# Attention of two layers: heads worked in pairs, with the values as stationary operand in two column tiles and the division by the row sums moved ahead of the transpose to GpSimd

## The reference, cut to what matters

```
for layer in range(2):
    h = rms_norm(x, g_mix[layer]);  qkv = h @ w_in[layer]
    o_a = differential_attention(...)   # 4 heads: a = softmax(q1 k1) - lam * softmax(q2 k2); o = a @ v, normed per head
    o_b = moba_attention(...)           # 4 heads, computed here as plain causal attention
    o_c = dilated_attention(...)        # 8 heads, computed here with an additive log-count mask ("strip")
    x = x + concatenate([o_a, o_b, o_c]) @ w_out[layer]
    x = x + conv_gated_mlp(...)
```

## Time and profile before

| what | value |
|---|---|
| median of 3 runs | 2205.19 us (2205.01 to 2206.89) |
| the profiled execution's own time | 2204.52 us |
| its span | 2202.7 us |
| PE busy | 2150.4 us, 98% |
| DVE / ACT / POOL busy | 1501.5 / 946.7 / 1197.0 us |
| attention of the first of the two layers | 1024.7 to 1130.0 us from the span's start |
| attention of the second | 1674.9 to 1780.1 us |
| granted PE clock | 0.996 of 2.4 GHz over the span |

### The profile page before, as it was taken

One profiled execution on the slowest core, in us unless ns is written; L12 is line 12 of the kernel. 1 busy time (PEld: TensorE's weight loads), 2 busy tenths in 40 slices (PEclk: granted clock), 3 DMA queues, 4 the chain that ended last, 5 costly groups with the idle time before them and its releaser, 6 DMA issues.

```text
span 2202.7 us, 33160 instructions
## 1 busy us (share of the span) xinstructions
PE 2150.4 (98%) x12377; PEld 1837.3 (83%) x12377; DVE 1501.5 (68%) x2234; ACT 946.7 (43%) x1891; POOL 1197.0 (54%) x594
## 2 busy tenths in 40 slices
PE   6999999999999999999999999999999999999997
PEld 4787888787899988897887898888897887888886
DVE  6844877654666692897737677677996728777676
ACT  3264663112465600645744555412555725555312
POOL 4766404765576677654026545577653037544675
PEclk9999999999999999999999999999999999999998
DMA  8322103422232343232002232322221012223221
GB/s 324 152 77 96 58 21 115 172 96 77 77 114 99 115 158 115 78 114 77 1 20 79 94 115 77 115 96 95 96 97 58 1 39 85 92 93 115 96 96 58
DMA packets 32776, 206.78 MB, mean 94 GB/s; under 512 B 4080, under 2 KB 4336, under 8 KB 11632
## 3 DMA queue, kind: packets, MB, share of 16 engines
q1 hardware_dynamic: 32192, 200.27, 24.8%
q10 hardware_dynamic: 432, 4.46, 0.5%
HBM read 202.61 MB, written 2.10 MB: 93 GB/s over the span
## 4 chain that ended last, share of the span: by engine, by line
PE 87%; DVE 6%; issue 1%; DMA 1%; ACT 1%; DVEq 1%; POOL 1%; POOLq 1%; SPq 0%; ACTq 0%
PE PS L1126 18%; PE PS L1128 18%; PE PS L1127 18%; PE PS L1605 5%; PE PS L1617 5%; PE PS L1381 3%; PE PS L1382 3%; PE PS L1383 3%; PE PS L1631 3%; PE PS L1457 2%; PE PS L1459 2%; PE PS L1458 2%; PE PS L1256 1%; PE PS L1259 1%; PE PS L1258 1%
## 5 line engine op out<-in xcount | busy, mean ns | idle before, releaser
L665 POOL TENSOR_TENSOR w_hi<-raw,zero_c 128x512 fp32r<-128x512 f32 (+1 forms) x135 | 281.6, 2104 | 536.0 <-PE PS L1128 534.5
L669 POOL TENSOR_TENSOR w_lo<-raw,w_hi 128x512 fp32r<-128x512 f32 (+1 forms) x135 | 366.2, 2731 | 5.8
L1126 PE MATMUL PS<-b_hi,w_hi 128*128 128x512 f32 x512 | 203.1, 397 | 0.9 <-POOL w_lo L888 0.9
L1127 PE MATMUL PS<-b_lo,w_hi 128*128 128x512 f32 x512 | 203.0, 396 | 0.0
L1128 PE MATMUL PS<-b_hi,w_lo 128*128 128x512 f32 x512 | 203.0, 396 | 0.0
L3346 DVE TENSOR_TENSOR b_lo<-a_all,b_hi 128x512 fp32r<-128x512 f32 x44 | 162.5, 3733 | 49.3 <-ACT b_hi L2491 49.3
L1126 PE MATMUL PS<-f_hi,w_hi 128*128 128x512 f32 x448 | 177.6, 397 | 0.7 <-DVE f_lo L2648 0.7
L1128 PE MATMUL PS<-f_hi,w_lo 128*128 128x512 f32 x448 | 177.6, 396 | 0.0
L1127 PE MATMUL PS<-f_lo,w_hi 128*128 128x512 f32 x448 | 177.6, 396 | 0.0
L688 POOL TENSOR_TENSOR w_lo<-raw,w_hi 128x512 fp32r<-128x512 f32 x48 | 71.0, 1478 | 90.5 <-ACT w_hi L2483 90.5
L1126 PEld LDWEIGHTS PS<-b_hi,w_hi 128*128 128x128 f32 x512 | 96.4, 188 | 24.6 <-POOL w_lo L888 1.1
(11 more groups left out here) (586 smaller groups left out, 6858.8 us busy)
## 6 DMA issues: line engine op xcount, KB each, us to landing
raw<-slabs_dram SPq DMA_DIRECT2D x161, 1024.0 KB, 4.8
aux<-ada_dram SPq DMA_DIRECT2D x18, 512.0 KB, 5.4
ada_first<-ada_dram SPq DMA_DIRECT2D x11, 512.0 KB, 14.0
cmpw<-cmpw_dram ACTq DMA_DIRECT2D x2, 2048.0 KB, 11.5
ada_late<-ada_dram SPq DMA_DIRECT2D x8, 512.0 KB, 3.2
ada_last<-ada_dram SPq DMA_DIRECT2D x8, 512.0 KB, 5.6
xT<-xT_dram SPq DMA_DIRECT2D x1, 2048.0 KB, 9.0
out_dram<-t SPq DMA_DIRECT2D x4, 512.0 KB, 3.2
```

Source lines behind the costliest of these rows:

```text
L665: high = nc.gpsimd.tensor_tensor(w_hi[:, slot, c], raw[:, slot, c], zero[:, 0:c.stop - c.start], ALU.add)
L669: low = nc.gpsimd.tensor_tensor(w_lo[:, slot, c], raw[:, slot, c], w_hi[:, slot, c].bitcast(f32), ALU.subtract)
L1126: nc.tensor.matmul(out, a_hi_, b_hi_, start=start, stop=False)
L1127: nc.tensor.matmul(out, a_hi_, b_lo_, start=False, stop=False)
```

## The change

Work is now laid out in units. A unit is a *pair* (the same block of queries of two plain or two dilated heads), a *diff* (the two score tiles of one differential head), a *turn* (two of the late turns of queries and keys) or *out* (the turns of the two 128-wide blocks of differential outputs). Each unit has two of four PSUM score banks; turns follow three units later, values four, the finish five. What happens to a pair:

- DVE takes the reciprocals of the two row sums as soon as both exponentials are there (`weigh`), and POOL multiplies both tiles of probabilities by them in place (`scale_pairs`), before the turn.
- PE turns both tiles; ACT copies the first and DVE the second.
- In the product with the values the values are now the stationary operand (64 columns) and the turned probabilities the moving one (128 columns). The first head's result goes to partitions 0 to 63, the second's to 64 to 127 of one bank: two column tiles. Features now lie on the partitions, so a group of two heads is a finished 128-wide block of `o_hi`/`o_lo` without another turn, and without `finish`.

Differential heads keep their product as it was, and the two blocks that they fill keep their turn. Their join is now made for each tile by itself. POOL splits the first two slabs of `w_out` during the attention, in pieces of 512 columns, one piece after the scaling of each pair but the first. The first slab's product with `w_out` (eight banks) begins, for four banks, between the last turns and values. Some pairs of semaphores are merged to make room; that is left out here.

```diff
+        LAG_T, LAG_V, LAG_OUT = 3, 4, 5
+        W_MASKED, W_PROBS, W_TURNED = 4, 8, 4
...
+        def two_units():
+            units, groups = [], [Group(n, b) for n, b in enumerate((4, None, 5, None, 0, 1, 2, 3))]
+            singles = {1: (8, 9), 2: (10, 11), 4: (12, 13), 5: (14, 15)}
+            for i in (0, 1):
+                for n, j in enumerate((3, 0, 2, 1)):
+                    units.append(Unit("pair", plain_jobs[2 * i:2 * i + 2], j, groups[2 * i]))
+                    for half in (0, 1):
+                        units.append(Unit("diff", diff_jobs[2 * i + half:2 * i + half + 1], j, groups[2 * i + 1], half))
+                    if 4 * i + n in singles:
+                        units.append(Unit("turn", items=singles[4 * i + n]))
+            for i in range(4):
+                for j in (3, 0, 2, 1):
+                    units.append(Unit("pair", dilated_jobs[2 * i:2 * i + 2], j, groups[4 + i]))
+            units.insert(DIFF_AT + 7, Unit("out", items=(6, 7)))
...
+            def pieces_of(n):                                        # POOL
+                pool.wait_ge(slab_loaded[slot], 16 * nth + 16)
+                pool.wait_ge(slab_used, n - 1)
+                for a in range(0, SLAB, PIECE):
...
+            def scale_pairs(n, plan, layer):                         # POOL
+                pieces = itertools.chain(pieces_of(n), pieces_of(n + 1))
+                for u in plan.units:
+                    if u.kind != "pair":
+                        continue
+                    pool.wait_ge(inverted, plan.pairs * layer + u.pair + 1)
+                    inv = pair_inv(u)
+                    for c in (0, 1):
+                        p = w_probs(u.score + c, 128 * u.nb)
+                        last = nc.gpsimd.tensor_scalar(p, p, inv[:, c:c + 1], None, ALU.mult)
+                    last.then_inc(scaled_probs, 1)
+                    if u.pair > 0:
+                        next(pieces, None)
...
+                def values(u):                                       # PE
+                    pe.wait_ge(copied_act, at_.acopies + u.on_act)
+                    if u.kind == "pair":
+                        pe.wait_ge(copied_dve, at_.dcopies + u.on_dve)
...
+                    for b in range(u.nb):
+                        if u.kind == "pair":
+                            for c in (0, 1):
+                                last = nc.tensor.matmul(PS[64 * c:64 * c + 64, bank, 128 * u.j:128 * u.j + 128],
+                                                        u.jobs[c]["v"](u.lo + b),
+                                                        w_turned(u.tile + c, 512)[:, 128 * b:128 * b + 128],
+                                                        start=b == 0, stop=b == u.nb - 1)
...
+                for t in range(len(plan.units) + LAG_V):             # PE
+                    u = plan.at(t)
+                    if u is not None:
+                        front(u)
+                    else:
+                        tail(t - len(plan.units))
+                    for lag, part in ((LAG_T, turns), (LAG_V, values)):
...
+                def weigh(u):                                        # DVE
+                    dve.wait_ge(probs_ready, g0 + u.score + 2)
+                    a = sum_at(u, 0)
+                    if u.kind == "pair":
+                        V.reciprocal(pair_inv(u), SUMS[:, a:a + 2]).then_inc(inverted, 1)
+                        return
...
+                    then(V.reciprocal(r, SUMS[:, b:b + 1]))
+                    then(V.scalar_tensor_tensor(out=r, in0=r, scalar=lam_c, in1=SUMS[:, a:a + 1], op0=ALU.mult,
+                                                op1=ALU.mult))
+                    V.scalar_tensor_tensor(out=two, in0=two, scalar=r, in1=one, op0=ALU.mult, op1=ALU.add
+                                           ).then_inc(combined, 1)
```

More of the change, by code:

```diff
@@ L19 @@
+import itertools
 import math
@@ L556, in build, with __init__ @@
         block = ctx.enter_context(nc.Block())
+        class Place:
+            def __init__(self):
+                self.meets = self.slab = self.drain = self.norms = self.bank = 0
+                self.tile = self.value = self.map = self.pair = self.acopies = self.dcopies = 0
+                self.turn = self.turn_a = self.turn_d = self.part = self.ffn = self.conv = 0
+                self.x = self.free = self.pairs = self.roots = self.mixes = self.folds = 0
+                self.pvs = self.scaled = 0
@@ L1643, in _, with woven @@
+            def woven(plan):
+                at_.tile += plan.scores
+                at_.value += plan.tiles
+                at_.pvs += plan.values
+                at_.pair += plan.joins
+                at_.scaled += plan.pairs
+                at_.map += plan.groups
+                at_.acopies += plan.on_act
+                at_.dcopies += plan.on_dve
             meet()
@@ L3541, in _ @@
-                o2_low(KD - 1, 3)
-                at_.turn += KD
-                at_.turn_a += KD
+                        dve.drain().then_inc(diff_dve, 1)
+                    u = plan.at(t - LAG_T)
+                    if u is not None and u.kind == "pair":
+                        copy(u)
+                    u = plan.at(t - LAG_OUT)
+                    if u is not None and u.last:
+                        finish_group(u)
+                at_.tile += plan.scores
+                at_.value += plan.tiles
```

788 lines of the change are left out of this document (500 added, 288 removed).

## The result

| kernel | median | runs | ratio to before, 95% interval |
|---|---|---|---|
| before | 2205.22 us | 2205.01 to 2206.89 (4) | |
| changed | 2221.29 us | 2219.34 to 2223.04 (4) | 1.0076 (1.0064 to 1.0088) |

What follows compares the result with a forecast made beforehand. PE, busy 98% of the span, was the bound; after the change DVE's front would pace the first part. Per layer 95.4 + 4.8 + 5.5 + 1.0 = 106.7 us against 105.7, so 2207 us, range 2194 to 2219.

Steps and rivals of the forecast that it cites:

- one of the rivals: DVE clearly the bound in the first part, every join waiting for POOL: +5.6 us a layer, 2217; chance 0.28.
- PE's own work: PE per layer: output turns -2.6 us, pairs' values -2.4 us, from 100.4 to 95.4.
- The rival that column tiles would not overlap: Pairs' values on PE in short stretches: 0.107 per record, +12 us a layer on PE, about 2225; chance 0.04.
- Hidden beside scores: Dilated part: DVE's copy of a pair's second tile costs nothing, made two to three steps before its bank is wanted.
- The wait of 4.8 us: First part, per layer: DVE's 58.6 us against PE's 53.8, so DVE's front sets the pace and PE waits 4.8.
- start and jitter: Per layer: 5.5 us idle for start and norm, 1.0 for units of uneven size.
- POOL's hold-up of DVE: First part: join operations with two SBUF operands wait for the running POOL instruction, 10.6 us for both halves.
- POOL's scale: POOL beside each pair: 1.0 us per 512-column scale, between 0.69 and 1.44, taken to block DVE.
- The parts: Attention of one layer: first part, plain and differential heads, 58 to 60 us; dilated part 48 to 49.

Runs made afterwards that it cites:

- e14: Changed kernel with ACT making both copies of turned probabilities, its copy placed ahead of the exponentials: 2207.19 us, ratio 1.0009.
- e16: As e15, but turns four units behind the scores and values one behind the turns: 2195.78 us, ratio 0.9961.
- e8: Changed kernel with the value product doing all blocks of the first head, then all of the second, without alternating column tiles: 2228.17 us, ratio 1.0107.
- e6: Changed kernel with DVE's copy of the second tile put ahead of the reciprocal or join of the same step: 2216.08 us, ratio 1.0046.
- e5: Changed kernel with ACT making both copies of a pair's turned tiles, none on DVE: 2213.39 us, ratio 1.0038.
- e9: Changed kernel with both copies on ACT, values five units behind, six places for turned probabilities, and a one-tensor small join operation: 2209.29 us, ratio 1.002.
- e15: As e9, with ACT's copies placed ahead of the exponentials: 2202.47 us, ratio 0.9992.
- e12: As e9, but turns four units behind the scores instead of three, values one behind the turns: 2226.2 us, ratio 1.0092.
- e13: Changed kernel with only ACT's copy moved ahead of the exponentials, DVE's copy left in place: 2221.86 us, ratio 1.0074.
- e11: As e9, but the second copy stays on DVE, placed ahead of the join: 2219.72 us, ratio 1.0071.
- e2: Changed kernel with the scale of probabilities moved from POOL to DVE, right behind the reciprocal: 2237.18 us, ratio 1.0148.
- e4: Changed kernel with the join's small operation reading one tensor and two per-partition scalars instead of two tensors: 2218.44 us, ratio 1.0066.
- e1: Changed kernel with POOL's scale left out, outputs not divided by row sums, pieces kept: 2219.65 us, ratio 1.0068.
- e10: As e9, with POOL's scale also left out: 2207.58 us, ratio 1.0012.
- e3: Changed kernel with the eight pieces of `w_out` split beside pairs 9 to 16, all dilated: 2241.04 us, ratio 1.0165.
- e7: Changed kernel with values five units behind the scores instead of four, finish six, six places for turned probabilities: 2212.93 us, ratio 1.0037.

## Why the prediction was wrong

The time was 2221, the forecast 2207 with a range to 2219. Slower was one of the rivals (2217; its own sum gives 2216), but by another mechanism.

Per layer the forecast was +1.0: 5.0 less work of PE and 6.0 more idle time (11.3 where 5.3 were). Measured are +8.3: PE busy 1.6 less, idle 9.9 more. So of the 7.3 us that the sum missed 3.9 are waits and 3.4 are PE's saving, which shows in full only in e14 and e16, where the granted clock was 1.00.

**PE's own work: right.** I gave 0.057 per record, 0.35 per stretch, six output turns gone, 5.0 us a layer less. The rows show 0.055 and about 0.25 to 0.3. PE busy, at a clock of 1.00, went from 148.1 to 143.0 (e14) and 142.1 (e16), 5 to 6 less. The saving is there and is seen in full where the clock stays at 1.00. The rule of the Trainium skill that a change of tiling mode drains the array (TensorEngine Tiling (Array Packing), Key Properties) agrees with the time lost at each stretch, at a price that the gain carries. The rival that column tiles would not overlap is out: e8's sixteen records without alternation are the slower ones.

**"Hidden beside scores": this step failed.** "A second tile's copy on DVE must be done two to three steps before its bank is wanted again; I cost it at nothing" took a copy to be as early as its data. It is as early as the place in its engine's in-order list. Behind the masks and the join of the newer units it is ready only when those are, and PE's next turn or values wait. I counted amounts (24.0 of DVE's 26.9 us) instead of following one step through the three engines. The wait of 4.8 us, for a DVE with 58.6 us of work in the first part, was not what came: DVE was busy for 48.3 of 63.2 us there, hold-ups included. Idle time came to 13.0 and 12.2 us a layer, where I had 4.8, and 5.5 and 1.0 for start and jitter, 11.3 together. That these sums lie near each other is chance: idle time before was 2.6 in the trace and 5.3 in my sum. What shows the place to be a cause are the pairs of runs that change nothing else: changed to e6 (2.8 less a layer by length), e5 to e14, e9 to e15 and e12 to e16 (3.1, 3.4 and 15.2 by the medians). Against them stands e13, which moves only ACT's copy and gains nothing while DVE's stays behind. (From e5 to e14 idle time falls by only 0.9; the rest is PE's busy time, at a higher clock.) From the changed kernel to e14 the length falls by 7.8 us, idle time by 4.3 and PE's busy time by 3.5, with POOL's scales and hold-ups all there (L3816 even has a mean of 518 ns in e14's first layer, 443 in the changed kernel's). But e14 also takes the second copies from DVE, some 10 us a layer, and e11 against e9 shows that the engine counts beside the place. How the gain divides over the two isn't shown.

**POOL's hold-up of DVE: real, and a minor term.** L3816 has a mean of 443 ns where it takes 220 alone. 32 by 0.22 us is 7.1 for two layers, 3.6 for one. The long operations add 1.0 in the first layer (four L3818 of 384 columns with a mean of 0.86 us, 0.62 in e2), so 4.6 where I had 10.6. It is visible in the first example and in e12's 1.78 us, and it costs time where work that PE needs stands behind it: about 1 a layer by e4, hardly clear of the spread, and 0.56 us instead of 2.71 at one and the same place of e16 and e12. The Trainium skill's statement that POOL shares its SBUF interfaces with DVE and contends with DVE instructions with two SBUF inputs (GPSIMD Engine Reference, Specifications) fits these rows, and did not decide the case.

**POOL's scale: mis-sized.** I took 1.0 us for 512 columns between 0.69 and 1.44; it is 1.56, above my dearest bound (a piece, at 2.4 by my sum, took 2.5). Leaving it out gave 0.8 us a layer as the kernel stood (e1) and 0.9 with the copies on ACT and more lag (e10), neither clear of the spread. It makes POOL nearly full in the dilated part, as e3 shows. And it is what PE waits for once the copies are out of the way: 4.8 of 13.0 us in the first layer of the changed kernel, 7.4 of 8.3 in e14, 5.1 of 6.2 in e15, and 1.5 of 4.4 in e16, whose turns follow one unit later. So e16's further gain, 3.3 us a layer on e15 by the medians, goes with this wait, though no run leaves out the scale there.

**The clock: no term of the sum.** In the changed kernel the granted clock was 0.95 and 0.96 in parts with waits (0.98 over the first layer's stretch), and 1.00 in the profiled executions of e14 and e16, whose waits are shorter. PE busy of 147.3 and 145.7 in two layers of the same work, at 0.98 and 0.99, against e14's 143.0 at 1.00, shows the size: 4.3 and 2.7 us. I had put this term at nothing, since the rows of before had 1.00 everywhere. It also differs from one execution to the next: over the whole span e14's ten have 0.993 (2210.85 and 2207.82 us) to 0.997 (2204.42, 2204.58 and 2206.24 us).

**The parts.** I gave 58 to 60 us for the first part; from 1025.68 to the first dilated score at 1088.87 it took 63.2. The dilated part, 48 to 49 by forecast, took 47.1 up to the first record of `w_out`, with the last turns and values woven into the product.

What stays open: how the 4.3 us between e14's idle time (8.2) and the changed kernel's divide over the copy's place and DVE's amount of work, why e11 lost what e6 and e7 gained, why e12 is so much slower than e9, and whether the kernel before would gain by the same order of copies; this wasn't tried. The comparison of e16 with the kernel before holds this advantage on one side only.

## What to carry to other kernels

On an in-order engine put work that frees a buffer for the bound engine ahead of work that waits for the newest input, if its own data are there by then (e11 is the warning). A longer lag of the turns cost 8.5 us a layer behind the wrong place (e9 to e12) and gave 3.3 behind the right one (e15 to e16). When work is regrouped into larger units, follow one whole step through all engines, as the loop score, mask, exponential, copy, next turn, and compare it with the bound engine's shortest step; busy shares would not show it. Here PE's saving of 5 us a layer did not show in the time until such loops were shorter than the step that it shortens. And where a change adds waits to the bound engine, give its clock a term of its own.

## What the runs showed of the hardware

A per-partition scale in place on POOL takes 0.60, 0.99, 1.24 and 1.56 us for 128, 256, 384 and 512 columns: dearer than POOL's subtraction of 512 columns (1.37 in the same kernel), though it reads one tensor; DVE takes 0.79 for the same 512 (e2). Float32 matmuls with a 64-column stationary operand and 128 moving columns, alternating between two column tiles, come at 0.055 us per record, with about 0.25 to 0.3 us for each stretch between full-width ones. The join's small operation on DVE, with two SBUF tensors, took 0.22 us at best and up to 1.01 beside POOL's instructions (L3816 of the changed kernel). In e4, with one tensor and two per-partition scalars, all 32 took 0.27 beside the same instructions.

Gaps in PE's work of 1 to 2 us went with a fall of the granted clock, but not each time. Windows of the changed kernel:

```profile
1112.50:1115.00 2.50, 1.10 (x9) 0.83 (x7) 2.38 (x2) 1.99 (x6) 2.06 (x2) 1.00 0.00 0
1115.00:1117.50 2.50, 1.41 (x10) 0.80 (x9) 1.53 (x8) 0.13 (x1) 0.00 (x0) 1.00 0.01 3
1117.50:1120.00 2.50, 2.50 (x7) 1.45 (x6) 1.45 (x7) 1.83 (x7) 2.28 (x2) 0.50 0.01 3
```

PE was busy for 2.5 of the 5 us, with gaps of 1.40 and 1.09, and then the granted clock was 0.50, the lower of its two levels (1.2 GHz). A score tile of four records of 384 columns that started at 1117.10 took 2.35 us until the next row, where it takes 1.39 at 1.00. Behind the gap of 1.67 of the first example (1050 to 1055, PE busy for 3.86 of 5.00) the clock stayed at 1.00.
